# Four column sums of the latents: one behind each quarter of the third slab, in place of all four behind the first quarter

## The chip, the core and the metric

The kernel runs on one core of a Trainium2 chip. The metric is device time in microseconds (us), the median of several executions. The engines are called as the profile calls them: PE is TensorE (matmuls; its weight loads are listed apart as PEld), DVE is VectorE, ACT is ScalarE, POOL is GpSimd, and SP is the queue that issues the weight DMAs.

## What is computed

The reference runs two blocks, one behind the other, on x of 512 tokens by 1024 channels, all float32. The first block has two layers (layer 0 and layer 1), and each begins with a mixer. Its start is what this change touches:

```python
h = rms_norm(x, g_mix_norm[l])
z = h @ w_in[l]
q_lat, kv_lat, k_rope = z[..., :o1], z[..., o1:o2], z[..., o2:o3]    # 256, 128 and 32 channels
...
q  = (rms_norm(q_lat, g_q_lat) @ w_q_up).reshape(B, S, MLA_HEADS, QK_HEAD)
kv = (rms_norm(kv_lat, g_kv_lat) @ w_kv_up).reshape(B, S, MLA_HEADS, QK_NOPE + V_HEAD)
...
q = rms_norm(q, g_q_head)
k = rms_norm(k, g_k_head)      # k is k_nope of its head beside the rotated k_rope
...
v = rms_norm(v, g_v)           # the 256 channels of the spatial gate's v
```

Each `rms_norm` needs, for each token, the sum of the squares over the channels. The channels of the latents lie on the partitions, so such a sum runs down a column: it is a matmul of the squares against a column of ones. Four are needed early: two tiles of q_lat (128 channels each), kv_lat (128 channels) and k_rope (32 channels).

## The kernel before

**Layout.** x lies as 8 tiles of 128 channels by 512 tokens. Weights come in slabs of 1 MB (128 x 2048), 216 in all. For each slab, SP loads it into one of two stage buffers; POOL writes a rounded high part (L381, one instruction) and the rest as a low part (L385, four instructions of 128 x 512), and PE takes three matmuls for a product (L443 high by high, L444 low by high, L445 high by low). POOL may split slab n only when PE has finished slab n - 2, since there are two weight buffers.

**Order.** There is no scheduler. Every engine runs a program that is written out by hand, in order, and semaphores join them. `mix(p)` on PE is the stage in question, run once in each layer. It takes these slabs:
- Slabs 1 and 2 of the phase: the latents into PSUM banks 0 to 3, then `turn_rstd`, which turns the norm of x so that DVE can copy it out of bank 6 (L1403). That copy frees bank 6 (semaphore `drained[6]`).
- Slab 3: the gate's v, in four quarters `c` of 128 tokens, into banks 4 and 5. A quarter is 24 matmuls of 256 columns. Behind quarter 0 stand the four `narrow_sum` calls.
- Slab 4: q, k and v from the latents (4 q tiles of 6 matmuls, 4 k tiles and 4 v tiles of 3 matmuls). Eight more `narrow_sum` calls stand between these tiles, the first behind the second q tile.
- Slabs 5 and 6, then attention. Slab 5 is followed by `spread` (L725), which uses factors from DVE.

**`narrow_sum`** (L653) waits until ACT has written a tile of squares (semaphore `narrow_squares`), does four one-column matmuls of it into bank 6, and counts up `narrow_summed`. In the records a one-column matmul of float32 stands as two, so a sum is 8 records.

**ACT** in this stretch: for the latents j = 0, 1, 2 and then k_rope, a square (L1060), each followed by a copy out of PSUM (L979; L1080 for k_rope). The squares use two buffers in turn, so square n waits for n - 1 finished sums (`narrow_summed`). Then four squares of the gate's v, one for each quarter (L1086), then two small square roots (L1065), the first of which waits for the first step of `var_ready` and the second for the second. Only then comes the square of the first q tile (L1060), and its copy (L1103).

**DVE** in this stretch: low parts of the latents (L1427) with the copy of the norm (L1403, L1433) between, the rotation of k_rope (L1396 to L1399), then a wait for the four sums. Behind it: a copy of the sums out of PSUM (L1445), two small tensor_tensor (L1447, L1448), L1449, which steps `var_ready`, and L1451. Then L1454, which also waits for the four squares of the gate's v and steps `var_ready` again. Then L1456 to L1464, more small steps on 128 x 4 and 128 x 8 numbers. These lines, from L1447 on, but for the two reciprocals, read two operands from SBUF. Each step waits for the one ahead of it, but for L1451, which is issued right behind L1449. Behind them stand the gate's v (L1468), the rotation of the four q tiles, and the factors (L1483 to L1497) for `spread`; after these L1501 reads slab 5's results.

Of the kernel before, what the change touches and what calls it, by code (L numbers as in the profile page):

```python
# [32 lines left out]
P = 128  # L33
# [15 lines left out]
TOK = T // P  # L49
# [104 lines left out]
def build(nc, a):  # L154

    ctx = ExitStack()
    with ctx:
# [282 lines left out]
        def _(pe):  # L440
            def triple(out, wa, wb, ra, rb, start, stop):

                pe.matmul(out, wa, ra, start=start, stop=False)  # L443
                pe.matmul(out, wa, rb, start=False, stop=False)  # L444
                return pe.matmul(out, wb, ra, start=False, stop=stop)  # L445
# [10 lines left out]
            def take(p, b):  # L456

                at_least(pe, drained[b], p.drain[b] + used[b])
                used[b] += 1
# [188 lines left out]
            def narrow_sum(rows, at):  # L648

                n = narrow[0]  # L650
                pe.wait_ge(narrow_squares, n + 1)
                for c in range(TOK):
                    last = pe.matmul(ps[:, 6, at + c:at + c + 1], W[rows, n % 2, c * P:(c + 1) * P], ones[rows, 0:1],  # L653
                                     start=True, stop=True)
                last.then_inc(narrow_summed, 1)
                narrow[0] += 1

            def mix(p):
# [8 lines left out]
                for c in range(TOK):  # L667
                    if c % 2 == 0:
                        take(p, 4 + c // 2)
                    out = ps[:, 4 + c // 2, (c % 2) * 256:(c % 2) * 256 + 256]  # L670
                    for k in range(8):
                        ha, la = xh[:, k, c * P:(c + 1) * P], xl[:, k, c * P:(c + 1) * P]
                        hb, lb = wh[:, s, k * 256:(k + 1) * 256], wl[:, s, k * 256:(k + 1) * 256]
                        last = triple(out, ha, la, hb, lb, k == 0, k == 7)
                    last.then_inc(tile_done if c < 3 else slab_done, 1)
                    if c == 0:

                        take(p, 6)
                        for n, rows in enumerate([slice(0, P), slice(0, P), slice(0, P), slice(64, 96)]):
                            narrow_sum(rows, TOK * n)  # L680

                s = (s0 + 3) % 2
                pe.wait_ge(slab_split, s0 + 4)
# [224 lines left out]
            pe.wait_ge(ones_set, 1)  # L908
            pe.wait_ge(const_landed, 32)
            programs = dict(mix=mix, ffn=ffn, conv=conv, mlp=mlp, ple=ple, attn=attn, final=final)  # L910
            for p in PHASES:
                start_phase(p)
# [915 lines left out]
```

## Time and profile before

| | us |
|---|---|
| median of 3 runs | 2730.27 |
| the three runs | 2731.31, 2727.86, 2730.27 |
| the profiled execution | 2729.78 |
| its span | 2728.0 |
| PE busy | 2618.1 (96%) |
| POOL busy | 1665.9 (61%) |
| DVE busy | 1271.9 (47%) |
| ACT busy | 471.6 (17%) |
| mean granted clock of PE | 0.981 |

The span is what the trace covers. A line of the profile names engine, source line, operation, what is written and read, and the count. The granted clock of PE is 1.00 at 2.4 GHz and 0.50 at 1.2 GHz. The mix phase of layer 0 lies near the start of the span; its third slab ends at 65.41 us. That of layer 1 ends its third slab at 621.88 us. These two times are when the first matmul of slab 4 starts.

### The profile page before, as it was taken

The numbers are of one execution on the slowest core, as the hardware profiler recorded it, in microseconds if no ns is written. First come the engines' busy times: TensorE is split into PE (matmuls) and PEld (weight loads), VectorE is DVE, ScalarE is ACT, GpSimd is POOL, SyncE is SP. The second block draws the span as 40 slices with busy tenths as digits, with TensorE's granted clock in tenths as the row PEclk, the third lists the DMA queues.
The fourth block names the chain that finished last, engine by engine and source line by source line (L and its number), as shares of the span: only waits on it lengthen the run. The fifth ranks groups of instructions, "written<-read, shape, count | busy, mean of one in ns | idle before, by whom it ended". The sixth has DMA issues, their size and how long they took to land.

```text
span 2728.0 us, 31488 instructions
## 1 busy us (share of the span) xinstructions
PE 2618.1 (96%) x11906; PEld 2145.6 (79%) x11906; DVE 1271.9 (47%) x1678; ACT 471.6 (17%) x777; POOL 1665.9 (61%) x1113
## 2 busy tenths in 40 slices
PE   7889999999899999999999999899999999999997
PEld 6668888877578888787888887688788878888885
DVE  5855443046654440345630514883367246604326
ACT  3332111023421110100100102300310043100012
POOL 4526677664276776666776766676337625767763
PEclk9989999999899999999999999999999999999998
DMA  4102222231022222222232233122112211232221
GB/s 151 62 19 92 106 92 93 102 107 60 16 93 103 97 92 94 91 97 89 101 107 93 92 106 103 66 104 92 62 47 92 95 45 70 93 108 92 93 92 62
DMA packets 36891, 236.70 MB, mean 87 GB/s; under 512 B 4048, under 2 KB 5584, under 8 KB 9168
## 3 DMA queue, kind: packets, MB, share of 16 engines
q1 hardware_dynamic: 33456, 230.78, 24.2%
q10 hardware_dynamic: 3360, 4.85, 0.5%
q8 instruction: 56, 0.92, 0.1%
q14 instruction: 19, 0.16, 0.0%
HBM read 233.51 MB, written 2.10 MB: 86 GB/s over the span
## 4 chain that ended last, share of the span: by engine, by line
PE 89%; DVE 7%; issue 2%; ACT 1%; POOL 0%; DMA 0%; DVEq 0%; SPq 0%; POOLq 0%; ACTq 0%
PE psum L443 28%; PE psum L444 27%; PE psum L445 27%; PE psum L891 2%; DVE work L1268 1%; DVE x_low L1284 1%; PE psum L875 1%; PE psum L653 1%; PE psum L900 1%; PE psum L763 1%; PE psum L779 0%; PE psum L472 0%; DMA x_res<-in_x 0%; POOL w_low L385 0%; DVE stat L1571 0%
## 5 line engine op out<-in xcount | busy, mean ns | idle before, releaser
L385 POOL TENSOR_TENSOR w_low<-w_stage,w_high 128x512 fp32r<-128x512 f32 x864 | 1214.8, 1437 | 18.0
L381 POOL TENSOR_SCALAR w_high<-w_stage 128x2048 fp32r<-128x2048 f32 x216 | 419.8, 1944 | 1008.7 <-PE psum L445 997.3
L443 PE MATMUL psum<-x_high,w_high 128*128 128x512 f32 x2048 | 806.3, 394 | 34.2 <-DVE x_low L1284 32.6
L444 PE MATMUL psum<-x_low,w_high 128*128 128x512 f32 x2048 | 799.6, 390 | 0.0
L445 PE MATMUL psum<-x_high,w_low 128*128 128x512 f32 x2048 | 799.2, 390 | 0.0
L443 PEld LDWEIGHTS psum<-x_high,w_high 128*128 128x128 f32 x2048 | 386.0, 188 | 121.4 <-issue 31.0
L444 PEld LDWEIGHTS psum<-x_low,w_high 128*128 128x128 f32 x2048 | 386.2, 189 | 82.8 <-issue 2.4
L445 PEld LDWEIGHTS psum<-x_high,w_low 128*128 128x128 f32 x2048 | 386.0, 188 | 80.3
L1308 DVE TENSOR_TENSOR x_res<-psum,x_res 128x512 f32<-128x512 f32 x64 | 47.1, 735 | 414.1 <-PE psum L445 414.1
L443 PE MATMUL psum<-mlp_high,w_high 128*128 (+1 forms) x576 | 224.8, 390 | 2.8 <-DVE mlp_low L1374 2.8
L444 PE MATMUL psum<-mlp_low,w_high 128*128 (+1 forms) x576 | 224.8, 390 | 0.0
L445 PE MATMUL psum<-mlp_high,w_low 128*128 (+1 forms) x576 | 224.6, 390 | 0.0
L974 ACT ACTIVATE x_high<-x_res,cols_sb 128x512 fp32r<-128x512 f32 x80 | 61.2, 773 | 530.0 <-DVE x_res L1308 529.5
L443 PE MATMUL psum<-ffn_high,w_high 128*128 (+1 forms) x352 | 136.9, 389 | 0.0
L444 PE MATMUL psum<-ffn_low,w_high 128*128 (+1 forms) x352 | 136.9, 389 | 0.0
L445 PE MATMUL psum<-ffn_high,w_low 128*128 (+1 forms) x352 | 136.9, 389 | 0.0
L443 PEld LDWEIGHTS psum<-mlp_high,w_high 128*128 128x128 f32 x576 | 108.5, 188 | 25.9 <-DVE mlp_low L1374 3.3
L445 PEld LDWEIGHTS psum<-mlp_high,w_low 128*128 128x128 f32 x576 | 108.5, 188 | 22.5
L444 PEld LDWEIGHTS psum<-mlp_low,w_high 128*128 128x128 f32 x576 | 108.5, 188 | 22.5
L1002 ACT ACTIVATE mlp_high<-work 128x512 f32 x64 | 40.6, 634 | 457.0 <-DVE work L1344 457.0
L1268 DVE TENSOR_TENSOR work<-work 128x512 f32<-128x512 f32 x87 | 108.9, 1252 | 1.6 <-ACT work L936 0.3
L1284 DVE SCALAR_TENSOR_TENSOR x_low<-x_res,cols_sb,x_high 128x512 fp32r<-128x512 f32 x80 | 102.6, 1289 | 14.2 <-ACT x_high L974 14.2
(240 smaller groups left out, 3045.1 us busy)
## 6 DMA issues: line engine op xcount, KB each, us to landing
w_stage<-in_wstream SPq DMA_DIRECT2D x216, 1024.0 KB, 4.8
x_res<-in_x SPq DMA_DIRECT2D x2, 1024.0 KB, 11.8
out_x<-attn_out SPq DMA_DIRECT2D x8, 256.0 KB, 2.1
inv_count_sb<-in_inv_count ACTq DMA_DIRECT2D x2, 512.0 KB, 8.6
ple_proj<-in_p ACTq DMA_DIRECT2D x2, 512.0 KB, 3.7
v_tok<-in_mask ACTq DMA_DIRECT2D x1, 576.0 KB, 3.8
w_spat<-in_spatial ACTq DMA_DIRECT2D x2, 256.0 KB, 5.3
diag_sb<-in_diag ACTq DMA_DIRECT2D x2, 256.0 KB, 9.4
```

Of the source, the lines that this page charges most:

```text
L381: pool.tensor_scalar(wh[:, s, :], stage[:, s, :], 1.0, 1.0, ALU.mult, ALU.mult).then_inc(high_written, 1)
L385: last = pool.tensor_tensor(wl[:, s, part], stage[:, s, part], wh[:, s, part].bitcast(F32), ALU.subtract)
L443: pe.matmul(out, wa, ra, start=start, stop=False)
L444: pe.matmul(out, wa, rb, start=False, stop=False)
L445: return pe.matmul(out, wb, ra, start=False, stop=stop)
L653: last = pe.matmul(ps[:, 6, at + c:at + c + 1], W[rows, n % 2, c * P:(c + 1) * P], ones[rows, 0:1], start=True, stop=True)
L891: last = pe.matmul(ps[:, b, r * P:(r + 1) * P], v, pt2[:, (n % 2) * 768 + kb * P:(n % 2) * 768 + (kb + 1) * P], start=kb == 0, stop=kb == 5)
L974: act.activation(dst, src, ACT.Copy, scale=gcol(p.gain + m)).then_inc(x_scaled, 1)
L1002: act.activation(hh2[:, bass.ds(i * 2 + m, 1), :].rearrange("p a t -> p (a t)"), W[:, 6 + m, :], ACT.Copy).then_inc(hidden_high, 1)
L1268: tt(W[:, ACC, :], W[:, ACC, :], src, ALU.add).then_inc(squares_added, 1)
L1284: dve.scalar_tensor_tensor(out=dst, in0=src, scalar=gcol(p.gain + m), in1=high, op0=ALU.mult, op1=ALU.subtract).then_inc(x_low, 1)
L1308: tt(dst, src, dst, ALU.add).then_inc(drained[m], 1)
```

## The change

The block of four calls behind quarter 0 goes, and one call stands behind each quarter. `take(p, 6)`, the wait for bank 6, stays behind quarter 0. The sums, their buffers and their order among themselves are the same, and the programs of the other engines are not touched.

```diff
                     last.then_inc(tile_done if c < 3 else slab_done, 1)
                     if c == 0:
-
                         take(p, 6)
-                        for n, rows in enumerate([slice(0, P), slice(0, P), slice(0, P), slice(64, 96)]):
-                            narrow_sum(rows, TOK * n)
+                    narrow_sum(slice(0, P) if c < 3 else slice(64, 96), TOK * c)
```

On PE, behind quarter 0 of the third slab in layer 0 (`w_high,x_high` are the quarter's matmuls, `ones,work` those of a sum; the lines without a sign stand in both):

```order
 L653 MATMUL psum<-ones,work 128x1 [waits narrow_squares,drained6]
 L653 MATMUL psum<-ones,work 128x1 x3
-L653 MATMUL psum<-ones,work 128x1 [waits narrow_squares]
-L653 MATMUL psum<-ones,work 128x1 x3
-L653 MATMUL psum<-ones,work 128x1 [waits narrow_squares]
-L653 MATMUL psum<-ones,work 128x1 x3
+L443 MATMUL psum<-w_high,x_high 128x256
+L444 MATMUL psum<-w_low,x_high 128x256
+L445 MATMUL psum<-w_high,x_low 128x256
```

The first sum stays where it was, and the matmuls of quarter 1 follow it at once.

On PE, the end of the third slab in layer 0 (`lat_high` and `lat_low` are the latents, read by the first q tile of slab 4):

```order
-L443 MATMUL psum<-w_high,x_high 128x256
-L444 MATMUL psum<-w_low,x_high 128x256
-L445 MATMUL psum<-w_high,x_low 128x256
+L653 MATMUL psum<-ones,work 128x1 [waits narrow_squares]
+L653 MATMUL psum<-ones,work 128x1 x3
 L443 MATMUL psum<-lat_high,w_high 128x512 [waits drained0,split_low,slab_split]
 L444 MATMUL psum<-lat_low,w_high 128x512
```

The fourth sum, that of k_rope, has moved behind the last matmul of quarter 3, and so stands between slab 3 and slab 4.

## Rows read from the trace of the kernel before

**Rows 1.** The page: busy time of each engine, and the chain that ended last.
```profile
PE 2618.1 (96%) x11906; PEld 2145.6 (79%) x11906; DVE 1271.9 (47%) x1678; ACT 471.6 (17%) x777; POOL 1665.9 (61%) x1113
...
PE 89%; DVE 7%; issue 2%; ACT 1%; POOL 0%; DMA 0%; DVEq 0%; SPq 0%; POOLq 0%; ACTq 0%
```

**Rows 2.** Timeline, PE, the four sums: start us, us, engine, line, operation.
```profile
45.93 0.28 PE L445 MATMUL psum<-w_high,x_low 128*128 128x256 f32 x1
48.29 7.07 PE L653 MATMUL psum<-ones,work 128*128 128x1 f32 x32 [2.08 <-DVE token_cols L1403]
55.29 0.58 PE L443 MATMUL psum<-w_high,x_high 128*128 128x256 f32 x1
...
607.80 4.13 PE L653 MATMUL psum<-ones,work 128*128 128x1 f32 x32
611.86 0.58 PE L443 MATMUL psum<-w_high,x_high 128*128 128x256 f32 x1
```

**Rows 3.** Stretches: us, busy of PE, PEld, DVE, ACT, POOL; PEclk, DMA share, GB/s.
```profile
48.29:55.29 7.00, 7.00 (x33) 6.97 (x33) 3.27 (x6) 2.44 (x4) 1.81 (x2) 0.50 0.43 150
55.29:58.23 2.94, 2.94 (x14) 2.94 (x14) 1.60 (x7) 0.00 (x0) 0.00 (x0) 0.50 0.00 0
58.23:65.41 7.18, 7.18 (x60) 7.18 (x60) 0.00 (x0) 1.06 (x4) 0.00 (x0) 0.99 0.01 2
607.80:611.30 3.50, 3.36 (x32) 3.28 (x30) 0.75 (x1) 2.40 (x4) 3.50 (x4) 1.00 0.00 0
611.86:614.80 2.94, 2.94 (x14) 2.94 (x14) 2.65 (x6) 0.00 (x0) 0.01 (x1) 0.50 0.59 176
```

**Rows 4.** Timeline, PE, slab 4 of layer 0: a sum between two q tiles.
```profile
71.19 0.39 PE L445 MATMUL psum<-lat_high,w_low 128*128 128x512 f32 x1
71.42 0.95 PE L653 MATMUL psum<-ones,work 96*128 96x1 f32 x8
72.23 0.47 PE L443 MATMUL psum<-lat_high,w_high 128*128 128x512 f32 x1
72.55 0.39 PE L444 MATMUL psum<-lat_low,w_high 128*128 128x512 f32 x1
```

**Rows 5.** Timeline, all engines, layer 1: from the sums to the first q square.
```profile
608.85 0.60 ACT L1060 ACTIVATE work<-psum 128x512 f32<-128x512 f32 x1 [7.27 <-PE psum L653]
...
614.64 0.16 DVE L1447 TENSOR_TENSOR token_cols<-token_cols 128x4 f32<-128x4 f32 x1
...
622.23 1.91 POOL L381 TENSOR_SCALAR w_high<-w_stage 128x2048 fp32r<-128x2048 f32 x1 [10.37 <-PE psum L445]
...
623.23 0.92 DVE L1454 TENSOR_TENSOR token_cols<-token_cols 128x4 f32<-128x4 f32 x1 [7.96 <-ACT work L1086]
...
624.18 0.30 ACT L1065 ACTIVATE token_cols<-token_cols,cols_sb 128x4 f32<-128x4 f32 x1 [0.88 <-DVE token_cols L1454]
624.22 4.99 POOL L385 TENSOR_TENSOR w_low<-w_stage,w_high 128x512 fp32r<-128x512 f32 x4
624.30 1.22 DVE L1459 TENSOR_TENSOR token_cols<-token_cols 128x4 f32<-128x4 f32 x1
624.39 0.57 ACT L1060 ACTIVATE work<-psum 96x512 f32<-96x512 f32 x1
...
625.11 1.02 PE L653 MATMUL psum<-ones,work 96*128 96x1 f32 x8 [0.32 <-ACT work L1060]
```

**Rows 6.** Timeline, DVE, small steps ahead of `spread`, beside POOL's L385.
```profile
647.49 0.60 DVE L1489 SCALAR_TENSOR_TENSOR token_cols<-token_cols 128x16 f32<-128x16 f32 x1
648.02 0.16 DVE L1491 TENSOR_TENSOR token_cols<-token_cols 128x16 f32<-128x16 f32 x1
648.22 1.15 DVE L1492 TENSOR_TENSOR token_cols<-token_cols 128x16 f32<-128x16 f32 x1
```

**Rows 7.** Stretches: slabs 4 and 5 by layer, and two parts of them.
```profile
82.39:85.24 2.85, 2.85 (x7) 1.81 (x6) 2.71 (x4) 0.72 (x2) 0.00 (x0) 0.50 0.00 0
638.75:648.90 10.15, 10.15 (x28) 7.85 (x27) 9.34 (x17) 3.67 (x5) 4.02 (x3) 0.50 0.00 0
65.41:98.18 32.77, 32.01 (x163) 26.04 (x162) 28.09 (x52) 16.09 (x29) 14.30 (x10) 0.95 0.16 50
621.88:657.44 35.56, 35.24 (x162) 28.47 (x161) 28.98 (x52) 14.80 (x28) 13.90 (x10) 0.86 0.17 59
```

**Rows 8.** Timeline, layer 0: the first q sum's wait, then DVE and PE at `spread`.
```profile
69.08 1.02 PE L653 MATMUL psum<-ones,work 96*128 96x1 f32 x8 [0.76 <-ACT work L1060]
69.97 0.48 PE L443 MATMUL psum<-lat_high,w_high 128*128 128x512 f32 x1
...
96.10 0.68 DVE L1501 TENSOR_TENSOR sgu_u<-psum,rstd 128x512 f32<-128x512 f32 x1
...
98.18 3.86 PE L725 MATMUL psum<-ident,probs_t 128*96 128x128 f32 x32
```

## The prediction

> **What bounds the kernel now.** First the page's busy times and the chain that ended last [rows 1]: PE is busy for 96% of the span and carries 89% of the chain, so work that PE does not do, or does not wait for, is worth a microsecond each. Second the timeline of PE around the four sums [rows 2]. In layer 0 PE waits 2.1 us for DVE to free bank 6 and then spends 48.29 to 55.29, 7.0 us, on the sums; in layer 1 it spends 607.80 to 611.86, 4.06 us. Third the stretches with their clock [rows 3]. In layer 0 the sums run at a granted clock of 0.50 (1.2 GHz), and so do the 14 matmuls behind them, 2.94 us; in layer 1 the sums start at 2.4 GHz, and the 14 matmuls behind them run at 1.2 GHz. PE was busy in both stretches of sums, but with one-column matmuls; at such work the clock fell in layer 1 and did not rise in layer 0. Fourth, the timeline of the four engines between the sums and the first q square of slab 4 [rows 5], because the change moves DVE's small steps to where POOL is at work.
>
> I call T the time at which slab 3's last matmul has been issued: in the kernel before, slab 4's first matmul starts there, 65.41 in layer 0 and 621.88 in layer 1.
>
> **Term A, slab 3 up to T.** What is removed is the block. One sum between dense matmuls costs about 0.90 us at 2.4 GHz: from 71.42 to 72.23 for the sum, and the first matmul behind it takes 0.32 us to the next in place of 0.23 [rows 4]. The four in a row in layer 1 took 4.06 us, so 0.46 us of that was waiting and pace, part of it for squares that ACT could start only when an earlier sum had gone (608.85 [rows 5]). With the change, squares 3 and 4 are made while PE does a quarter. A quarter is 24 matmuls; 60 took 7.18 us, so a quarter is 2.87 us at 2.4 GHz and 24 x 0.21 = 5.04 us at 1.2 GHz (14 in 2.94) [rows 3].
> Layer 1: before, 607.80 to 621.88 is 14.08 us. After: three quarters, 8.61, and three sums, 2.70, together 11.3. The gain is 2.8 us, 1.3 of it the 14 matmuls that now keep 2.4 GHz.
> Layer 0: before, 48.29 to 65.41 is 17.12 us. The wait for bank 6 stays, and with it the 1.2 GHz at its end. After: one sum at 1.2 GHz, 7.00 / 4 = 1.75; quarter 1 at 1.2 GHz, 5.04; two quarters, 5.74; two sums, 1.80; together 14.3. The gain is 2.8 us; it would be 3.7 if the clock rose after 14 matmuls again.
> Term A is -5.6 us.
>
> **Term B, from T to the first q sum of slab 4.** The fourth sum now stands behind T, so PE reaches the first q sum at T + 0.9 + 2.75 (12 matmuls at 0.23) = T + 3.65. Before, it waited there for ACT's first q square and started at T + 3.67 in layer 0 and T + 3.23 in layer 1 [rows 5, 8]. If ACT's square came as before, the fourth sum would be nearly free. It does not, by this reading. ACT makes that square behind two roots, the second of which waits for L1454, and L1454 stands behind L1445 to L1451, which wait for the fourth sum. Before, that chain ran while POOL was idle, and L1447 took 0.16 us. L1454 ran while POOL was in L381 and took 0.92, ending when POOL's instruction ended (624.15 and 624.14); L1459, beside L385, took 1.22, about one of L385's four pieces (4.99 / 4 = 1.25) [rows 5]. POOL starts L381 when slab 3 is done, at T + 0.35, and is busy to T + 7.3. So the whole chain moves under POOL.
> Step by step in layer 1: the fourth sum starts at T; an engine that waits for a sum started 1.05 us after its start (607.80, 608.85 [rows 2, 5]); L1445 reads PSUM, 0.17; L1447 then waits for the end of L381, T + 2.27. L1448 comes 0.04 later, and POOL's first piece of L385 starts 0.08 after L381. Either L1448 goes first (case a) and takes 0.16, L1449 ends with POOL's first piece, L1451 slips in behind it as L1491 did (0.16 right behind L1489 [rows 6]), and L1454 ends with the second piece, near T + 4.95; or L1448 waits for a piece too (case b) and L1454 ends near T + 6.1. L1454 ended at 624.15 before and PE's first q sum started at 625.11, 0.96 later. That gives PE T + 5.9 in a and T + 7.1 in b. I take a, because the row of L1491 shows a step that goes through in such a gap. PE starts the first q sum 2.7 us later after T than before in layer 1 and 2.2 in layer 0. Term B is +4.9 us (a) or +7.3 (b).
> The Trainium skill ("SBUF — State Buffer", section "Who interferes with whom") states that a DVE instruction with two SBUF inputs contends with a GpSimd instruction that reads SBUF, and that the later to issue fully blocks until the first ends. The rows agree: 0.92 and 1.22 us against 0.16. It speaks against this change; at 0.16 us a step, which holds only with POOL idle, term B would be +0.4.
> What is queued behind the waits: ACT's q squares and copies, and DVE's chain up to the factors. DVE has some room: its last factor copy is done about 2 us before PE reaches `spread` (96.10, 98.18 [rows 8]), and PE is delayed more than DVE is, since DVE's steps L1456 to L1464 then run when POOL has finished. The rotation of k_rope also comes one quarter later, 3 us of DVE, hidden by quarters 2 and 3. SP's and POOL's work shifts with slab 3's end and covers itself.
>
> **Term C, the clock.** With B, PE issues no wide matmul from T + 3.65 to T + 6.8 (case a) or T + 8.0 (case b): a wait and a sum, 3.2 to 4.3 us. The nearest rows: 4.06 us of sums in layer 1, after which the clock was down; 2.3 us idle in layer 0 (to 48.29), likewise [rows 2, 3]; and in layer 0's slab 4 some 1.8 us (wait and sum, to 69.97 [rows 8]), after which the matmuls kept 2.4 GHz. So I expect a fall in both layers. Then slab 4 goes on with short groups of matmuls and a sum behind most of them, and the same slab shows what that does: 1.2 GHz lasted for 2.85 us in layer 0 and for 10.15 us in layer 1, up to the dense matmuls of slab 5 [rows 7]. Its price: slabs 4 and 5 took 32.77 us in layer 0 (clock 0.95, so 3.3 us at half) and 35.56 in layer 1 (0.86, so 10.0), with a first wait 0.44 shorter in layer 1; (2.79 + 0.44) / 6.7 is about 0.48 us for each us at 1.2 GHz. The bounds are 0, no fall, and a stay at 1.2 GHz from T + 6 until slab 5, which would be some 23 us more per layer and cost 11. I take layer 1's length, about 9.5 us more at half than before in each layer: 4.5 us each. Term C is +9 us.
>
> **Sum.** -5.6 + 4.9 + 9.0 = +8.3 us. On the profiled execution, 2729.8 us, that is 2738.1; against the median, 0.5 us higher, 2738.6. I give 2738.6 us.
>
> **Rivals.**
> - The clock holds or recovers at once (C near 0 to 2). For it: layer 0's 2.85 us, and a fall that each layer already has late in slab 4 may go away in exchange. Against it: the length of the gap. A + B + C is then -0.7 to +3.7, about 2731.5: no change.
> - Faster: DVE's steps aren't held up. If POOL's instructions leave more gaps than L1454 and L1459 show, or the steps slip in between, ACT's first q square comes by T + 3.65; B is then +0.4 us, the clock has no gap to fall in, and the sum is -5.2: 2725. It decides at L1454's end: up to T + 2.7 PE waits for nothing. For it: L1491. Against it: of the small steps beside POOL, L1454, L1459 and L1492 were each held, and four steps in a row would have to get through.
> - Slower still: case b and 1.2 GHz through slab 4 in both layers: -5.6 + 7.3 + 22 = +24, 2754.
> That the change doesn't do what it says is ruled out by the order of PE's instructions.
>
> **How the numbers follow.** A measurement of this kernel can tell about 0.2%, 5.5 us, from no change. The forecast (waits, and a clock that falls) has 0.50, and with it the slower rival 0.12; the clock that holds 0.23; the faster rival 0.15. The forecast's own range is 2732 to 2748, and some 0.07 of its 0.50 lies within 0.2%. The faster rival lies at the edge: -5.2 with a spread of some 3 us from where the clock changes, so I give 0.08 of it to faster and 0.07 to the same; 0.03 of the holding clock goes to faster. This makes faster 0.11, same 0.34, slower 0.55. The range 2725 to 2752 leaves out about 0.1 on either side.
>
> **What would show each step.** A: in the new trace slab 3 takes 11.3 us from its first sum to T in layer 1 and 14.3 in layer 0, with three sums of 0.8 to 0.9 us apart in layer 1. B: L1447, L1449 and L1454 show about 1 us each beside POOL's L381 and L385, ACT's second root starts at T + 5 or later, and PE shows some 2 to 3.5 us of idle time before the first q sum. C: granted clock 0.50 behind that wait, over 10 us of slab 4 and 5 in each layer. The prediction fails if the steps show 0.16 us, or if the clock keeps 1.00 behind the wait; it is too low if slab 4 stays at 0.50 throughout in both layers.

## The result, and the profile after

| | before | changed |
|---|---|---|
| median of 18 runs, us | 2729.55 | 2734.70 |
| lowest and highest | 2727.09, 2733.68 | 2724.94, 2745.51 |
| the profiled execution | 2729.78 | 2734.31 |
| its span | 2728.0 | 2732.5 |

The ratio of the times is 1.0018, with a 95% interval from 1.0011 to 1.0025: the changed kernel is slower by 5.15 us (0.19%), clear of noise but small: it is just under the 0.2% that the prediction took for the least that can be told from no change, and with 18 runs it can be told. The scatter changed more than the median: 6.6 us before, 20.6 us after. Three of the 18 runs lie between 2724.9 and 2725.8, fourteen between 2732.8 and 2739.9, and one at 2745.5. Their mean granted clocks follow the same groups: 0.984 in the first three, 0.978 to 0.981 in the fourteen, 0.977 in the last.

**Slab 3** answers to [rows 2] and [rows 3]. Stretches of the changed kernel (us, busy of PE, PEld, DVE, ACT, POOL; PEclk, DMA share, GB/s), layer 0 and layer 1, each from the first sum to T:

```profile
48.29:61.26 12.97, 12.97 (x96) 12.84 (x97) 4.16 (x7) 3.51 (x8) 1.82 (x2) 0.87 0.24 82
605.34:616.73 11.39, 11.39 (x98) 11.26 (x96) 3.56 (x6) 3.51 (x8) 4.13 (x4) 1.00 0.27 94
```

Before, this stretch took 17.12 and 14.08 us with all four sums in it, so 4.15 and 2.69 us are gained here; the stretch now holds three sums, and the fourth stands behind T.

**Behind T** answers to [rows 5]. Timeline of layer 1, all engines but the dense matmuls:

```profile
616.73 1.05 PE L653 MATMUL psum<-ones,work 32*128 32x1 f32 x8
...
616.99 1.90 POOL L381 TENSOR_SCALAR w_high<-w_stage 128x2048 fp32r<-128x2048 f32 x1 [7.52 <-PE psum L445]
...
618.03 0.88 DVE L1445 TENSOR_TENSOR token_cols<-token_cols 128x4 f32<-128x4 f32 x1
618.94 0.16 DVE L1446 TENSOR_TENSOR token_cols<-token_cols 128x4 f32<-128x4 f32 x1
618.98 4.98 POOL L385 TENSOR_TENSOR w_low<-w_stage,w_high 128x512 fp32r<-128x512 f32 x4
619.13 1.16 DVE L1447 SCALAR_TENSOR_TENSOR token_cols<-token_cols 128x4 f32<-128x4 f32 x1
620.22 0.15 DVE L1449 TENSOR_TENSOR token_cols<-token_cols 128x4 f32<-128x4 f32 x1
620.40 1.13 DVE L1452 TENSOR_TENSOR token_cols<-token_cols 128x4 f32<-128x4 f32 x1
...
621.56 0.30 ACT L1063 ACTIVATE token_cols<-token_cols,cols_sb 128x4 f32<-128x4 f32 x1 [0.93 <-DVE token_cols L1452]
...
622.48 1.62 PE L653 MATMUL psum<-ones,work 96*128 96x1 f32 x8 [1.72 <-ACT work L1058]
```

The lines behind the edit have moved up by 2: L1445 here is L1447 before, L1447 is L1449, L1452 is L1454, L1063 is L1065. Where [rows 5] has a step of 0.16 us with POOL idle, the steps now run beside POOL's L381 and L385, and every second one takes about 1 us: L1445 ends with L381 (618.91, 618.89), L1446 goes through in the gap, L1447 and L1452 each last until the end of one of L385's pieces. ACT's second root then starts at 621.56, and PE, idle for 1.72 us, starts the first q sum at 622.48: T + 5.75, where it was T + 3.23. In layer 0 it is 61.26 and 67.28, T + 6.02, where it was T + 3.67.

**The clock behind that wait** answers to [rows 7]. First stretch: from the first q sum of layer 0 to `spread`. Second: layer 1, from 0.4 us behind the start of the first q sum.

```profile
67.28:94.85 27.57, 27.57 (x149) 22.93 (x150) 24.52 (x50) 12.73 (x21) 8.31 (x7) 1.00 0.19 65
622.90:650.02 27.12, 27.12 (x89) 22.06 (x89) 16.24 (x33) 9.64 (x18) 1.06 (x1) 0.50 0.11 39
```

Layer 0 kept 2.4 GHz from the first q sum to `spread`. Layer 1 fell to 1.2 GHz at about 622.8 and stayed there up to about 650.1, nearly to the end of slab 4 (slab 5's first matmul starts at 651.64): 27 us, where the kernel before had 10.15 behind T in that layer.

The start of `spread` (L725 before, L723 here) sums this up. The source line in layer 1 (count, durations in ns, first and last start):

```profile
L723 PE MATMUL psum<-ident,probs_t x32: 270/273/321, 662.5 to 666.1; 128*96 128x128 f32 x32
```

In layer 0 `spread` starts at 94.85, the end of the first stretch above, 3.3 us earlier than before (98.18 [rows 8]). In layer 1 it starts at 662.5, 5.1 us later than before (657.44, where the last stretch of [rows 7] ends). When layer 1's mixer begins, 2.4 us of layer 0's gain are left, so that mixer alone lost 7.5 us.

### The profile page after: what moved, and what is told of

The parts are those of the page before. It is cut to its first block, busy times and chain, and to the rows that moved or that the text cites. A ratio compares the mean times of both kernels' runs of the same rounds, so it can differ in the third digit from the quotient of the medians.

```text
span 2732.5 us, 31488 instructions
## 1 busy us (share of the span) xinstructions
PE 2621.8 (96%) x11906; PEld 2148.0 (79%) x11906; DVE 1271.4 (47%) x1678; ACT 471.9 (17%) x777; POOL 1664.7 (61%) x1113
## 4 chain that ended last, share of the span: by engine, by line
PE 89%; DVE 7%; issue 2%; ACT 1%; POOL 0%; DMA 0%; DVEq 0%; SPq 0%; POOLq 0%; ACTq 0%
PE psum L443 28%; PE psum L445 27%; PE psum L444 27%; PE psum L889 2%; DVE work L1266 1%; DVE x_low L1282 1%; PE psum L873 1%; PE psum L653 1%; PE psum L898 1%; PE psum L777 0%; PE psum L761 0%; PE psum L472 0%; DMA x_res<-in_x 0%; POOL w_low L385 0%; PE psum L723 0%
## 5 line engine op out<-in xcount | busy, mean ns | idle before, releaser
L385 POOL TENSOR_TENSOR w_low<-w_stage,w_high 128x512 fp32r<-128x512 f32 x864 | 1214.4, 1436 | 18.0
L381 POOL TENSOR_SCALAR w_high<-w_stage 128x2048 fp32r<-128x2048 f32 x216 | 419.5, 1942 | 1014.4 <-PE psum L445 1002.8
```

The costliest lines, as they stand in the source:

```text
L381: pool.tensor_scalar(wh[:, s, :], stage[:, s, :], 1.0, 1.0, ALU.mult, ALU.mult).then_inc(high_written, 1)
L385: last = pool.tensor_tensor(wl[:, s, part], stage[:, s, part], wh[:, s, part].bitcast(F32), ALU.subtract)
```

## The experiments

Theory: DVE's steps, held up by POOL, make PE's wait; the wait lets the clock fall; the fall costs more than the wait. Without it the change gains. Each run was timed beside the kernel before on the same chip. That was 2731.03 us (median of 25) for four runs: POOL's wait, ACT's roots in the changed kernel, the wide filler, and the fourth sum behind quarter 2. It was 2729.70 (16) for the narrow filler, the two kernels with two and two sums, and the roots in the kernel before. It was 2729.55 beside the changed kernel itself, so kernels of different groups are best compared by their distance to their own kernel before.

### POOL waits for DVE's steps

```diff
-                    split_run(at, p.slab + 8)
+                    split_run(at, p.slab + 4)
+                    pool.wait_ge(var_ready, 3 * p.layer + 2)
+                    split_run(p.slab + 4, p.slab + 8)
```

> The changed kernel, with one wait more: POOL starts the split of slab 5 of the mix phase only when DVE has stepped var_ready twice (behind L1454), so DVE's small steps run with POOL idle. Theory (POOL holds the steps up, and that makes PE's wait and the clock's fall): the steps take 0.16 to 0.2 us each, PE waits under 0.5 us before the first q sum in both layers, the clock has no gap to fall in there, slab 3's gain of about 5.6 us stays: 2724 to 2726 us against 2729.6 before, ratio 0.998, with little spread. Rival (the wait comes from the fourth sum's late place alone, whatever POOL does): PE still waits 2 us and the time stays near 2735.

Measured: 2722.89 us, ratio 0.9970 (0.9959 to 0.9981), 8.1 us under the median before. That is 1 us below the range expected, and the spread, 2718.08 to 2726.35, is not as little as expected. Timeline of this kernel, layer 1, DVE, POOL and PE (the sums are at L655):

```profile
613.15 1.05 PE L655 MATMUL psum<-ones,work 32*128 32x1 f32 x8
...
614.45 0.16 DVE L1447 TENSOR_TENSOR token_cols<-token_cols 128x4 f32<-128x4 f32 x1
614.64 0.17 DVE L1448 TENSOR_TENSOR token_cols<-token_cols 128x4 f32<-128x4 f32 x1
614.84 0.16 DVE L1449 SCALAR_TENSOR_TENSOR token_cols<-token_cols 128x4 f32<-128x4 f32 x1
...
615.11 0.16 DVE L1454 TENSOR_TENSOR token_cols<-token_cols 128x4 f32<-128x4 f32 x1
615.46 1.90 POOL L381 TENSOR_SCALAR w_high<-w_stage 128x2048 fp32r<-128x2048 f32 x1 [9.63 <-DVE token_cols L1454]
...
617.03 0.95 PE L655 MATMUL psum<-ones,work 96*128 96x1 f32 x8
```

The steps take 0.16 us again, and the first q sum starts at T + 3.88 with no idle time noted ahead of it (T + 3.87 in layer 0). Only POOL's start was moved. So POOL's work is what held the steps, and the late place of the fourth sum alone makes no wait: the rival of this run falls. PE's order is that of the changed kernel.

The clock still fell in this kernel, later in slab 4 of layer 1. The stretch in question, with PE busy all the time in it and in the 16 us ahead of it:

```profile
629.20:639.30 10.10, 10.10 (x31) 8.19 (x31) 7.83 (x17) 4.29 (x7) 1.69 (x1) 0.50 0.00 0
```

So a fall of the kernel before's length (10.15 us) in that slab needs no wait ahead of it. Late in slab 4 of layer 1 there is one of 7 to 10 us in the profiles of both kernels with only ACT's roots moved, of the wide filler, of the fourth sum behind quarter 2, and of the kernel with two and two sums. What came with the wait in the changed kernel is an earlier and much longer fall, and no profile of a kernel with that wait gone or filled with wide matmuls shows one of that length.

### ACT's roots behind the second q tile

```diff
-                narrow_root(p, 1, nar[:, 32:40], nar[:, 24:32], Q_LORA)
-                narrow_root(p, 2, nar[:, 72:76], nar[:, 68:72], 256)
...
                 for n in range(2 * HEADS):
...
+                    if n == 1:
+                        narrow_root(p, 1, nar[:, 32:40], nar[:, 24:32], Q_LORA)
+                        narrow_root(p, 2, nar[:, 72:76], nar[:, 68:72], 256)
```

> The changed kernel, with ACT's two small roots (L1065) moved behind the second q tile's square and copy, so that no q square waits for DVE's chain; DVE's steps still run beside POOL. Theory (PE is held up only through the roots that stand ahead of the first q square): PE's wait before the first q sum is gone, DVE's steps still show about 1.1 us each, time 2724 to 2726, ratio 0.998. Rival (the late DVE chain itself delays something further on, the copies of v or the factors for spread): PE waits there in place of here, and the time stays at 2729 or above.

Measured: 2724.38 us, ratio 0.9968 (0.9955 to 0.9981), as expected. Timeline of layer 0, PE and DVE:

```profile
62.82 1.05 PE L653 MATMUL psum<-ones,work 32*128 32x1 f32 x8
...
64.11 0.94 DVE L1446 TENSOR_TENSOR token_cols<-token_cols 128x4 f32<-128x4 f32 x1
65.09 0.16 DVE L1447 TENSOR_TENSOR token_cols<-token_cols 128x4 f32<-128x4 f32 x1
65.29 1.17 DVE L1448 SCALAR_TENSOR_TENSOR token_cols<-token_cols 128x4 f32<-128x4 f32 x1
...
66.56 1.13 DVE L1453 TENSOR_TENSOR token_cols<-token_cols 128x4 f32<-128x4 f32 x1
66.69 0.95 PE L653 MATMUL psum<-ones,work 96*128 96x1 f32 x8
```

DVE's steps are as slow as in the changed kernel (L1448 and L1453 here are its L1447 and L1452), but PE starts the first q sum at T + 3.87, while L1453 is still at work. The slow steps hurt only through the two roots that stood ahead of ACT's first q square.

### The roots moved in the kernel before

The same edit of ACT, with the block of four sums as before.

> The kernel before, block of four sums and all, with only ACT's two roots moved behind the second q tile. Theory (the roots' place matters only where DVE's chain is late, and here it is early): only the old waits of 0.76 and 0.32 us go, 2730 less about 1: 2729 to 2730.5, ratio 0.9995. Rival (moving the roots is worth by itself what the run on the changed kernel gained): 2725 or below.

Measured: 2727.86 us, ratio 0.9992 (0.9983 to 1.0001). That is 1.8 us by the medians, near the 1 us expected of the small waits, and it is not the 6 to 8 us of the two runs above. So those came from the sums' new places, once the wait was gone.

### PE's wait filled with wide matmuls

```diff
                     if h == 1:
+                        at_least(pe, drained[7], p.drain[7] + used[7])
+                        for _ in range(8):
+                            pe.matmul(ps[:, 7, :], wh[:, s, 0:P], lath[:, 0, :], start=True, stop=True)
                         take(p, 6)
```

> The changed kernel, with 8 matmuls of 512 columns into the unused bank 7 ahead of the first q sum (extra work, its result is overwritten later): they fill 1.8 us of PE's wait of 2 us and leave the wait's end where it is. Theory (the wait costs little in itself, the fall of the clock behind it costs the rest): the first q sum starts at the same distance behind slab 3, T + 5.8 to 6.0, the clock stays at 1.00 behind it, and the time is 2727 to 2730 in spite of 16 matmuls more, without runs above 2732. Rival (the clock falls anyway from the short groups and the sums between them): 2733 or above, granted clock 0.50 in slab 4 of at least one layer.

Measured: 2725.71 us, ratio 0.9988 (0.9978 to 0.9997); 9 of 12 runs lie between 2722.75 and 2727.54, three between 2732.05 and 2734.85. Timeline of layer 0 (its last line shows 7 of the sum's 8 records), then two stretches behind the first q sums of layer 0 and layer 1, and a later one of layer 1:

```profile
65.11 1.97 PE L691 MATMUL psum<-lat_high,w_high 128*128 128x512 f32 x8
67.28 0.91 PE L653 MATMUL psum<-ones,work 96*128 96x1 f32 x7 [0.19 <-ACT work L1061]
```

```profile
67.28:94.80 27.52, 27.52 (x148) 22.93 (x149) 24.53 (x50) 12.73 (x21) 8.37 (x7) 1.00 0.18 63
622.55:635.00 12.45, 12.45 (x77) 10.43 (x77) 11.92 (x27) 8.17 (x15) 1.50 (x2) 1.00 0.25 86
636.60:643.30 6.70, 6.70 (x20) 5.16 (x20) 4.41 (x11) 3.01 (x5) 1.43 (x1) 0.50 0.00 0
```

The first q sum starts where it did in the changed kernel (67.28), so the wait is the same length; it is only filled. The clock holds behind it in both layers: in layer 0 up to `spread`, in layer 1 for some 14 us, and then it falls for 6.8 us, late in slab 4. A kernel with 16 matmuls more has a median 9.0 us under that of the changed one (10.5 us when each is set against its own kernel before), and somewhat below the 2727 to 2730 expected. The wait in itself is the smaller part (2.8 us lie between this kernel and the one where POOL waits); the fall behind it is the larger. The three slower runs were not expected. Filling seems to make the slow pattern rarer and not to remove it; no profile of a slower run was taken.

### The same wait filled with one-column matmuls

```diff
                     if h == 1:
+                        at_least(pe, drained[7], p.drain[7] + used[7])
+                        for _ in range(9):
+                            pe.matmul(ps[:, 7, 0:1], ident[:], ones[:, 0:1], start=True, stop=True)
                         take(p, 6)
```

> The changed kernel, with 9 one-column matmuls (float32, 18 records) into the unused bank 7 ahead of the first q sum: the same 1.8 us of PE's wait filled as in the run before, but with narrow work. Theory (the clock follows wide matmuls, and one-column ones count as nearly idle): the clock falls as often as in the changed kernel, some runs near 2725, most between 2732 and 2740, median about 2734.7. Rival (any work on PE keeps the clock): median near 2725.7 as with the 8 wide matmuls, few runs above 2732.

Measured: 2738.78 us, ratio 1.0030 (1.0018 to 1.0042), all six runs between 2736.85 and 2740.36. Timeline of layer 0, then stretches of layer 1 from inside slab 4's first tiles to the first q sum, and behind it:

```profile
66.79 2.06 PE L691 MATMUL psum<-ones,ident 128*128 128x1 f32 x18
68.93 1.02 PE L653 MATMUL psum<-ones,work 96*128 96x1 f32 x8
```

```profile
623.00:628.20 5.20, 5.20 (x38) 4.71 (x36) 5.03 (x8) 2.11 (x6) 5.12 (x5) 1.00 0.00 0
628.80:636.00 7.20, 7.20 (x28) 6.16 (x27) 6.89 (x18) 1.99 (x5) 0.00 (x0) 0.54 0.42 148
```

PE is busy through the whole wait, and the clock falls behind it all the same in layer 1. In layer 0 of this profile it held behind the filler and fell later, at 82.3, for 10 us. Against the wide filler, with the first q sum at the same T + 6.0 in layer 0, the difference is 13 us (14 against each one's own kernel before). So PE being busy did not keep the clock here, and 8 wide matmuls in the same place did. That this kernel is slower than the changed one too, by some 4 us, was not expected. Its profile shows most of that: slab 3 of layer 0 was at 1.2 GHz for 6.8 us in place of 3.4 and took 14.5 us in place of 13.0, and from T to `spread` both layers lost by the clock, 38.3 and 42.8 us against 33.6 and 45.8 in the changed kernel's first profile. Why the fall came in both layers is open.

### The fourth sum behind quarter 2

```diff
                     if c == 0:
                         take(p, 6)
-                    narrow_sum(slice(0, P) if c < 3 else slice(64, 96), TOK * c)
+                    for n in {0: (0,), 1: (1,), 2: (2, 3)}.get(c, ()):
+                        narrow_sum(slice(0, P) if n < 3 else slice(64, 96), TOK * n)
```

> Sums 1 and 2 behind quarters 0 and 1 as in the changed kernel, sums 3 and 4 both behind quarter 2: the fourth sum is out of the way of slab 3's end, and DVE's steps run during quarter 3, while POOL is idle. Theory: the gain in slab 3 (about 5.6 us) without the wait behind it; steps at 0.16 us, PE waits for ACT's first q square as in the kernel before (0.3 and 0.8 us): 2724 to 2725, ratio 0.998. Rival (what costs is the interleaving itself, sums between dense quarters): no better than the changed kernel, 2733 to 2737.

Measured: 2726.71 us, ratio 0.9981 (0.9972 to 0.9990). Timeline of layer 1:

```profile
612.16 0.16 DVE L1446 TENSOR_TENSOR token_cols<-token_cols 128x4 f32<-128x4 f32 x1
612.35 0.16 DVE L1447 TENSOR_TENSOR token_cols<-token_cols 128x4 f32<-128x4 f32 x1
...
615.17 1.91 POOL L381 TENSOR_SCALAR w_high<-w_stage 128x2048 fp32r<-128x2048 f32 x1 [8.59 <-PE psum L445]
...
618.04 1.02 PE L653 MATMUL psum<-ones,work 96*128 96x1 f32 x8 [0.32 <-ACT work L1059]
```

The steps up to `var_ready`'s first are done before POOL starts. The one behind them (L1453 here, L1454 in the kernel before) waits for ACT's last square, 616.17, and takes 0.92 us beside POOL, as it did in the kernel before. The wait ahead of the first q sum is 0.32 us, also that of the kernel before. The gain is 4.3 us by the medians, with the time 2 us above the range expected. The fourth sum, 0.95 us in each layer, now stands ahead of T and does not fill the waits for ACT (0.76 and 0.32 us), which explains a part. Interleaving is a gain by itself; the rival falls.

### Two sums behind quarter 1, two behind quarter 2

```diff
-                    if c == 0:
+                    if c == 1:
                         take(p, 6)
-                    narrow_sum(slice(0, P) if c < 3 else slice(64, 96), TOK * c)
+                    for n in {1: (0, 1), 2: (2, 3)}.get(c, ()):
+                        narrow_sum(slice(0, P) if n < 3 else slice(64, 96), TOK * n)
```

> Sums 1 and 2 behind quarter 1, sums 3 and 4 behind quarter 2, none behind quarter 0. In layer 0 PE then has quarter 1 to do while DVE frees bank 6. Theory (the 2.1 us wait for bank 6 and the 1.2 GHz behind it are a cost of their own, still there in the changed kernel): slab 3 of layer 0 gains 2 us more and keeps 2.4 GHz, 1.3 us: 3 to 3.5 us under the run with the fourth sum behind quarter 2 (2726.7), so 2722 to 2724. Rival (two sums together, with their ACT squares in turn, wait for each other as the four did, and the third latent's low part comes too late for slab 4): PE waits 1 us behind quarter 2 or ahead of slab 4 and the time is 2726 or above.

Measured: 2719.05 us, ratio 0.9963 (0.9950 to 0.9977), all five runs between 2718.72 and 2721.29. Timeline of layer 0, and then the stretch from inside quarter 0 to the first q sum:

```profile
48.66 1.84 PE L653 MATMUL psum<-ones,work 128*128 128x1 f32 x16
50.36 0.36 PE L443 MATMUL psum<-w_high,x_high 128*128 128x256 f32 x1
...
53.32 1.93 PE L653 MATMUL psum<-ones,work 128*128 128x1 f32 x16
...
58.15 0.40 PE L443 MATMUL psum<-lat_high,w_high 128*128 128x512 f32 x1
```

```profile
46.00:61.80 15.80, 15.06 (x116) 14.21 (x115) 8.28 (x18) 7.97 (x20) 7.07 (x6) 1.00 0.21 68
```

PE no longer waits for bank 6, the clock stays at 1.00, and T of layer 0 is 58.15, against 61.26 in the changed kernel and 65.41 before. The gain over the run above, 7.7 us by the medians and 6.3 against each one's own kernel before, is more than the 3 to 3.5 us expected; the profile doesn't tell where all of it comes from, and the clock's scatter is part of any such difference.

With ACT's roots behind the second q tile as well:

> As the run before, with ACT's two roots behind the second q tile as well. Theory: each layer also loses the wait before the first q sum that the kernel before had (0.76 and 0.32 us), and the gaps in slab 4 are shorter, so the clock falls less often: 1 to 2 us under the run before, 2721 to 2723. Rival: ACT is late with the roots, DVE's factors come later and PE waits at spread: no gain or a loss.

Measured: 2718.23 us, ratio 0.9959 (0.9945 to 0.9973), below the 2721 to 2723 expected and the fastest here, 11.5 us under the kernel before; the two kernels' intervals overlap almost wholly, so the roots' part of it isn't shown.

### The changed kernel three times more

The kernel is the changed one, unedited; what is looked at is the clock.

> The changed kernel once more, for its clock. Theory (the wait is the same in each execution, and whether the clock falls behind it differs from execution to execution and from layer to layer): the first q sum starts 5.7 to 6.1 us behind slab 3's end in both layers again; the time goes with the layers that fell: about 2725 for none, 2732 to 2737 for one, 2742 to 2746 for two. Rival (layer 0 always holds and layer 1 always falls, from what surrounds them): clock 1.00 in slab 4 of layer 0 and 0.50 through slab 4 of layer 1, 2732 to 2740, in every one of these runs.

> As the run ahead of it: the same kernel, another execution. Theory: wait of the same length, another pattern of the clock is possible. Rival: the same pattern as in the profile at hand.

> As the two runs ahead of it: the same kernel, another execution. Theory: wait of the same length, another pattern of the clock is possible. Rival: the same pattern as in the profile at hand.

Measured: 2735.42, 2735.45 and 2732.63 us, beside 2729.51 for the kernel before. The first of them, layer 0: PE's timeline at the first q sum, the stretches before and behind it, and `spread` in both layers (first and last start):

```profile
67.15 1.53 PE L653 MATMUL psum<-ones,work 96*128 96x1 f32 x8 [1.99 <-ACT work L1058]
```

```profile
61.14:67.60 6.46, 4.47 (x25) 3.61 (x24) 5.17 (x9) 4.01 (x10) 6.06 (x5) 0.99 0.01 3
67.60:94.60 27.00, 27.00 (x89) 21.94 (x88) 15.99 (x33) 9.59 (x17) 0.81 (x1) 0.50 0.11 39
```

```profile
L723 PE MATMUL psum<-ident,probs_t x64: 270/273/321, 107.2 to 668.3; 128*96 128x128 f32 x64
```

The wait is the same to 0.02 us (T + 6.01), but here layer 0 fell, for 27 us. In layer 1 of this run the clock held behind the first q sum and fell only at about 647.8, for 6.8 us. The second and third runs show the same pattern, layer 0 from 67.6 and from 68.1. So in each of the four profiles of the changed kernel one layer fell behind the wait for 24 to 27 us and the other did not (at most 6.8 us later on), and not always the same one: the rival falls. The executions near 2725 and the one at 2745.5 would be those with no layer and with both. No profile of such a one was taken, but their mean clocks speak for it: 0.984, 0.980 and 0.977 of some 2730 us are about 87, 109 and 126 us at 1.2 GHz, an estimate, so about 20 us apart.
These runs also give a clean price: T to `spread` in layer 0 took 46.1 us here (61.14 to 107.2) and 33.6 in the changed kernel's first profile, with the same work and the same wait: 12.5 us for 27 us at 1.2 GHz, 0.46 each.

## Why the prediction was right, and which term was off

The forecast was +8.3 us against the profiled execution and 2738.6 us; measured are +5.15 by the medians and 2734.70. The mechanism was the one forecast, in each of its three terms; two of them were mis-sized, A by 1.2 us and C by 2.8 us.

- **Term A** was put at -5.6 us and measured -6.8. Layer 1's 11.39 us against 11.3 was right. In layer 0, 14.3 us was forecast and 12.97 measured: the step "one sum at 1.2 GHz ... quarter 1 at 1.2 GHz" failed, since in this execution the first sum still ran at 2.4 GHz (1.05 us) and the clock was back up inside quarter 1. The 2.1 us wait for bank 6 is the same (2.08 by [rows 2]; the 2.3 us of idle time that term C names there is the same wait, read too long), but the fall around it lasted 3.4 us in place of 10.2, and in one of the three later profiles of the changed kernel there was none.
- **Term B** was put at +4.9 us (case a) and measured +4.9: 2.35 in layer 0 and 2.52 in layer 1. The order of fast and slow steps was case a, one by one. The rule cited from the Trainium skill ("SBUF — State Buffer", section "Who interferes with whom") held where the traces could try it: the steps are slow beside POOL (changed kernel) and fast with POOL held back (the first experiment).
- **Term C** was put at +9.0 us, as 9.5 us more of 1.2 GHz in each of two layers. From T to `spread`, layer 0 took 33.59 us against 32.77, and layer 1 some 45.8 against 35.56, so 11.0 us in all; less B's 4.9, C is +6.2. The sum is right in size by two errors that go against each other: the step "I expect a fall in both layers" failed, only one fell behind the wait in each of four profiles; and the step "I take layer 1's length" failed, the fall lasted not 10 but 24 to 27 us, near what was given as the bound. That the sum came out near is luck: 19 us more at 1.2 GHz were forecast, and about 13.7 were measured (17.1 more in layer 1, 3.4 fewer in layer 0). The price for each us was right, 0.48 forecast and 0.46 measured.
- The sum of the three is +4.2; with 0.9 us lost in the rest of layer 0 and some 0.6 gained behind layer 1's `spread` it comes to the 4.5 us between the spans.

The rival "faster" priced the wait's absence at -5.2 us, 2725. With the wait taken away in two ways, the kernel took 2722.9 and 2724.4 beside 2731.0, so that price was somewhat low. The rival of a holding clock, put at about 2731.5, was measured near 2725.7 with the filler: too high. A was 1.2 us more of a gain, and C, put at 0 to 2, was -3.2 in the filler's profile (33.6 and 36.4 us from T to `spread`, less B's 4.9), since where the clock holds behind the wait, the later falls of the kernel before shrink as well: layer 0's of 3.4 us is gone, and layer 1's lasted 6.8 us in place of 10.2.

## What to carry to other kernels

Before small vector steps are moved to "later, where PE is dense", look at what POOL does there: of steps that read two SBUF operands, each may take as long as POOL's current instruction, and whoever waits for the end of such a chain waits for the sum. A wait of 2 us on PE cost 12 through the clock here, where what follows is short groups of matmuls with narrow ones between, and the clock did not come back among them for 24 to 27 us; so price a wait by what stands behind it, and allow for a fall among such groups even where nothing waits. And put work for which its inputs are early, like these sums, behind enough dense matmuls to cover the wait for its bank, and ahead of the point where another engine becomes busy.

## What the runs showed of the hardware that was not expected

- The clock at 1.2 GHz lasted 27 us at a stretch in which PE was busy all the time (27.12 of 27.12 us), and it rose at 650.1, near the end of slab 4, behind six matmuls of 512 columns in a row; three such groups of six ahead of it, with sums between, had not brought it back.
- A fall came without any wait too: in the kernel where POOL waits, PE was busy throughout, and layer 1 was at 1.2 GHz for 10 us from 629.2 on.
- The same kernel, with the same wait to 0.02 us, fell in layer 0 in three profiles and in layer 1 in one. What decides it in an execution is open; the scatter from 2724.9 to 2745.5 us fits it.
- What the prediction took from one row (L1491) held for a whole chain: a small DVE step that comes in the 0.09 us between two POOL instructions went through in 0.16 us, and the next one lasted to the end of a POOL instruction: fast and slow steps alternate (0.88, 0.16, 1.16, 0.15, 1.13 us).
